# The expert stage's sixteen slots: waiting slot by slot instead of by groups of four

## The reference, cut to what matters

```python
def one_block(args):
    hb, eb, gb = args
    a = jax.nn.gelu(jnp.einsum('td,thkd->thk', hb, u[eb]))
    return jnp.einsum('thk,thkd->td', (gb * a).astype(v.dtype), v[eb])
```

## Time and profile before

| | us |
|---|---|
| median of three runs | 5759.28 (5758.3 to 5764.06) |
| profiled execution, its own time | 5768.66 |
| its span, first to last instruction | 5766.5 |
| TensorE busy in the span | 4560.9 (79%) |
| VectorE busy | 2323.8 (40%) |
| GpSimd busy | 1169.3 (20%) |
| ScalarE busy | 886.2 (15%) |
| queue of the gathers (q0), its packets' time as a share of 16 engines' span | 46.0% |

### The profile page before, as it was taken

How to read it: one execution, slowest core, us unless ns; L and a number is a source line. 1 busy time by engine, 2 the same in 40 slices (tenths; PEclk the granted TensorE clock), 3 DMA queues, 4 the chain that set the end, 5 groups by cost and what they waited for, 6 DMA issues and landing times. The chain is left out here.

```text
span 5766.5 us, 41916 instructions
## 1 busy us (share of the span) xinstructions
PE 4560.9 (79%) x13011; PEld 2177.4 (38%) x13044; DVE 2323.8 (40%) x5481; ACT 886.2 (15%) x1951; POOL 1169.3 (20%) x1104
## 2 busy tenths in 40 slices
PE   6999999977777767888837777777777777777777
PEld 1444444434544543344312333333333333333333
DVE  2000000003333334388894554454544445454544
ACT  1100000012222220121101111111111111111111
POOL 0000000000000000000004444444444444444443
PEclk8999999987777776899977888888888898889888
DMA  7143444462101023311009999999999999999997
GB/s 260 53 156 136 149 156 156 166 208 92 42 35 57 31 76 136 140 47 47 28 3 367 411 409 412 405 402 400 407 401 401 407 408 412 408 411 410 410 405 313
DMA packets 247745, 1409.28 MB, mean 244 GB/s; under 512 B 24467, under 2 KB 76179, under 8 KB 110804
## 3 DMA queue, kind: packets, MB, share of 16 engines
q0 software_dynamic: 148896, 1083.11, 46.0%
q1 hardware_dynamic: 72118, 272.53, 13.4%
q10 hardware_dynamic: 26672, 52.88, 2.4%
HBM read 1341.66 MB, written 159.08 MB: 260 GB/s over the span
## 5 line engine op out<-in xcount | busy, mean ns | idle before, releaser
L1677 DVE CUSTOM_DVE_ANT_0 ex_UV<-ex_UV,ex_h 128x1024 f32<-128x1024 f32 x1024 | 1194.0, 1221 | 1211.9 <-DMA ex_UV<-in_peer_uv,ex_idx 1211.9
L1546 POOL DMA_INDIRECT ex_UV<-in_peer_uv,ex_idx x1024 | 1135.0, 1108 | 1534.5 <-PE ex_acc L1591 630.5
L1591 PE MATMUL ex_acc<-ex_UV,ex_diag 128*128 128x512 f32 x2048 | 1015.8, 659 | 320.2 <-ACT ex_diag L1617 320.2
L1591 PE MATMUL ex_bc<-ex_UV,ex_diag 128*128 128x512 f32 x2048 | 1008.9, 656 | 318.1 <-ACT ex_diag L1617 318.1
L406 PE MATMUL z_ps<-win,hT 128*128 128x464 f32 x2688 | 1055.2, 554 | 22.3 <-ACT z_stage L383 11.6
L1591 PEld LDWEIGHTS ex_acc<-ex_UV,ex_diag 128*128 128x128 f32 x2048 | 429.3, 213 | 905.8 <-issue 526.6
L1591 PEld LDWEIGHTS ex_bc<-ex_UV,ex_diag 128*128 128x128 f32 x2048 | 425.9, 211 | 899.7 <-issue 519.6
L406 PEld LDWEIGHTS z_ps<-win,hT 128*128 128x128 f32 x2688 | 510.9, 191 | 555.9 <-issue 537.4
L763 DVE TENSOR_SCALAR mx_gn<-mx_gn 128x1024 f32<-128x1024 f32 x1 | 0.7, 694 | 1136.8 <-DMA mx_gn<-in_gla_gn_g 1136.8
L1534 POOL DMA_INDIRECT ex_UV<-in_peer_uv,ex_idxT x8 | 7.6, 953 | 1740.9 <-DVE ex_idxT L1646 1738.8
L1612 ACT ACTIVATE ex_u<-ex_u 128x8 f32<-128x8 f32 x128 | 26.7, 209 | 2130.0 <-DVE ex_u L1449 2130.0
(11 more groups left out here) (332 smaller groups left out, 3399.5 us busy)
## 6 DMA issues: line engine op xcount, KB each, us to landing
out_kv_w_sample<-in_cache_kv_w SPq DMA_DIRECT2D x8, 8188.0 KB, 42.7
win<-in_w_in SPq DMA_DIRECT2D x21, 1856.0 KB, 11.4
z_scratch<-z_stage ACTq DMA_DIRECT2D x21, 1856.0 KB
ada<-in_ada_w SPq DMA_DIRECT2D x12, 2048.0 KB, 7.8
ex_UV<-in_peer_uv,ex_idx POOLq DMA_INDIRECT x1024, 8.5
out_kv_w_sample<-in_cache_kv_w SPq DMA_DIRECT2D x8, 2044.0 KB, 18.1
mx_zg<-z_scratch SPq DMA_DIRECT2D x8, 1544.0 KB, 7.1
mx_zq<-z_scratch SPq DMA_DIRECT2D x8, 1536.0 KB, 10.1
```

The costliest lines, as they stand in the source:

```text
L1546: pool.indirect_dma_start(out=UV[n][:, :], out_offset=None, in_=uv_dram, in_offset=bass.IndirectOffsetOnAxis(ap=idx[b][:, n:n + 1], axis=0 ...
L1591: last = nc.tensor.matmul(acc[:, b, :], dg[:, n, :], V[n][:, b * 512:(b + 1) * 512], start=False, stop=False)
L1677: nc.vector.tensor_tensor_reduce(out=U[n], in0=U[n], in1=hb, scale=1.0, scalar=0.0, op0=ALU.mult, op1=ALU.add, accum_out=a[:, n:n + 1]).th ...
```

## The change

The landing semaphores become sixteen, one per slot. GpSimd waits before every gather for one more slot to be summed. VectorE waits before every dot and TensorE before every sum for that slot's own landing. Names `NBUF` (16), `ROUNDS` (`NSLOT // NBUF`, 1), `SUB` (8) and `SUBS` (2) replace literal values; buffers are addressed as `n % NBUF`.

```diff
-    GRP = 4
-    NQ = NSLOT // GRP
-    HALF = NSLOT - NS
+    NBUF = 16
+    ROUNDS = NSLOT // NBUF
+    HALF = NBUF - NS
...
-    loaded = [k.sem(f"ex_rows_loaded{q}") for q in range(NQ)]
+    loaded = [k.sem(f"ex_slot_loaded{n}") for n in range(NBUF)]
...
-    SUB = NSLOT // 2
+    SUB = 8
+    SUBS = NSLOT // SUB
...
                     for n in range(NSLOT):
-                        if n % GRP == 0:
-                            pool.wait_ge(p["vdone"], (i * PH + h) * NSLOT + n + GRP)
-                            pool.sem_inc(p["zero"], 1)
-                        pool.indirect_dma_start(out=UV[n][:, :], out_offset=None, in_=uv_dram,
-                                                in_offset=bass.IndirectOffsetOnAxis(ap=idx[b][:, n:n + 1], axis=0)).then_inc(loaded[n // GRP], 16)
+                        pool.wait_ge(p["vdone"], (i * PH + h) * NSLOT + n + 1)
+                        pool.sem_inc(p["zero"], 1)
+                        pool.indirect_dma_start(out=UV[n % NBUF][:, :], out_offset=None, in_=uv_dram,
+                                                in_offset=bass.IndirectOffsetOnAxis(ap=idx[b][:, n:n + 1], axis=0)).then_inc(loaded[n % NBUF], 16)
...
-                            if n % GRP == 0:
-                                pe.wait_ge(loaded[n // GRP], (i * PH + h) * (16 * GRP) + 16 * GRP)
+                            pe.wait_ge(loaded[n % NBUF], ((i * PH + h) * ROUNDS + n // NBUF) * 16 + 16)
...
-                            if n % GRP == 0:
-                                dve.wait_ge(loaded[n // GRP], (i * PH + h) * (16 * GRP) + 16 * GRP)
+                            dve.wait_ge(loaded[n % NBUF], ((i * PH + h) * ROUNDS + n // NBUF) * 16 + 16)
...
-                        at_least(dve, p["diag"], (i * PH + h) * NSLOT + c * SUB - SUB)
+                        at_least(dve, p["diag"], (i * PH + h) * NSLOT + c * SUB + SUB - NSLOT)
```

More of the change, by code:

```diff
@@ L1462, in experts @@
     rows_s = [k.sem(f"ex_rows_sample{n}") for n in range(NS)]
-    loaded = [k.sem(f"ex_rows_loaded{q}") for q in range(NQ)]
+    loaded = [k.sem(f"ex_slot_loaded{n}") for n in range(NBUF)]
     uv_dram = k.i["peer_uv"]
-    SUB = NSLOT // 2
+    SUB = 8
+    SUBS = NSLOT // SUB
     with k.phase() as f:
-        UV = [f.sb(f"ex_UV{n}", [P, 2 * D]) for n in range(NSLOT)]
+        UV = [f.sb(f"ex_UV{n}", [P, 2 * D]) for n in range(NBUF)]
         U = [t[:, 0:D] for t in UV]
@@ L1576, in _ @@
                 pe.wait_ge(s["s_sum"], 1)
-                pe.sem_inc(p["vdone"], NSLOT - HALF)
+                pe.sem_inc(p["vdone"], NBUF - HALF)
                 pe.wait_ge(s["tiles_done"], 2)
@@ L1586, in tile @@
                         for n in range(NSLOT):
-                            if n % GRP == 0:
-                                pe.wait_ge(loaded[n // GRP], (i * PH + h) * (16 * GRP) + 16 * GRP)
+                            pe.wait_ge(loaded[n % NBUF], ((i * PH + h) * ROUNDS + n // NBUF) * 16 + 16)
                             pe.wait_ge(p["diag"], (i * PH + h) * NSLOT + n + 1)
                             for b in range(2):
-                                last = nc.tensor.matmul(acc[:, b, :], dg[:, n, :], V[n][:, b * 512:(b + 1) * 512], start=False, stop=False)
+                                last = nc.tensor.matmul(acc[:, b, :], dg[:, n, :], V[n % NBUF][:, b * 512:(b + 1) * 512], start=False, stop=False)
                             last.then_inc(p["vdone"], 1)
@@ L1609, in head @@
                 def head(i, h):
-                    for c in range(2):
-                        act.wait_ge(p["g_u"], (i * PH + h) * 2 + c + 1)
+                    for c in range(SUBS):
+                        act.wait_ge(p["g_u"], (i * PH + h) * SUBS + c + 1)
                         nc.scalar.activation(uu[:, c * SUB:(c + 1) * SUB], uu[:, c * SUB:(c + 1) * SUB], ACT.Tanh, scale=GELU_C).then_inc(p["g_exp"], 1)
-                        act.wait_ge(p["w"], (i * PH + h) * 2 + c + 1)
+                        act.wait_ge(p["w"], (i * PH + h) * SUBS + c + 1)
                         for n in range(c * SUB, (c + 1) * SUB):
@@ L1671, in head @@
                 def head(i, h, hb):
-                    for c in range(2):
+                    for c in range(SUBS):
                         cols = slice(c * SUB, (c + 1) * SUB)
                         for n in range(c * SUB, (c + 1) * SUB):
-                            if n % GRP == 0:
-                                dve.wait_ge(loaded[n // GRP], (i * PH + h) * (16 * GRP) + 16 * GRP)
-                            nc.vector.tensor_tensor_reduce(out=U[n], in0=U[n], in1=hb, scale=1.0, scalar=0.0, op0=ALU.mult, op1=ALU.add,
+                            dve.wait_ge(loaded[n % NBUF], ((i * PH + h) * ROUNDS + n // NBUF) * 16 + 16)
+                            nc.vector.tensor_tensor_reduce(out=U[n % NBUF], in0=U[n % NBUF], in1=hb, scale=1.0, scalar=0.0, op0=ALU.mult, op1=ALU.add,
                                                            accum_out=a[:, n:n + 1]).then_inc(p["dotted"], 1)
@@ L1680, in head @@
                         dve.sem_inc(p["dots_done"], SUB)
-                        link = chained(dve, p["g_steps"], (i * PH + h) * 6 + c * 3)
+                        link = chained(dve, p["g_steps"], ((i * PH + h) * SUBS + c) * 3)
                         gelu_steps(nc, link, a[:, cols], t[:, cols], uu[:, cols]).then_inc(p["g_u"], 1)
-                        dve.wait_ge(p["g_exp"], (i * PH + h) * 2 + c + 1)
+                        dve.wait_ge(p["g_exp"], (i * PH + h) * SUBS + c + 1)
                         link(nc.vector.scalar_tensor_tensor(out=t[:, cols], in0=uu[:, cols], scalar=1.0, in1=a[:, cols], op0=ALU.add, op1=ALU.mult))
                         gate = k.gate[:, bass.ds(i * P + h * NSLOT + c * SUB, SUB)]
-                        at_least(dve, p["diag"], (i * PH + h) * NSLOT + c * SUB - SUB)
+                        at_least(dve, p["diag"], (i * PH + h) * NSLOT + c * SUB + SUB - NSLOT)
                         nc.vector.scalar_tensor_tensor(out=w[:, cols], in0=t[:, cols], scalar=0.5, in1=gate, op0=ALU.mult, op1=ALU.mult).then_inc(p["w"], 1)
```

## The result

| | before | after |
|---|---|---|
| median | 5761.42 us (5758.3 to 5764.06, 4 runs) | 5681.43 us (5674.33 to 5687.88, 4 runs) |
| ratio | | 0.9861, 95% interval 0.9844 to 0.9878 |
| profiled execution, span | 5768.66, 5766.5 | 5674.33, 5672.2 |
| first gather of the stage to the last instruction | 2739.9 us | 2645.3 us |

The changed kernel is 1.4% faster. The prediction said 5668 (5648 to 5722). Run beside another kernel later, it had 5678.03 (5 runs) against 5767.32 (9 runs) before, ratio 0.9846 (0.9826 to 0.9865).

A forecast was written before the change was run, and what follows sets the result against it. Gathers bound the expert stage, losing 94 us to a short queue. From 5768.66 us: -94, 6 given back, -3 at the end, giving 5678; the median lies 9.4 us below that execution, so 5668 us (5648 to 5722).

The forecast's parts named there:

- What bounds it: Expert stage, 3100 to 5730 us: gathers move 407 GB/s against 422 with a filled queue; 94 us lost.
- (1) to (3): Finer refill and landing waits: first refill issued 7.7 us into a turn instead of 17.9, reserve 11.2 us, gaining 94 us.
- T: Instant in one turn of the loop when VectorE starts on the last group of a half's slots as its landing is seen.
- (4): Price of the added waits, 768 each on VectorE, TensorE and GpSimd: taken as 0, being met or covered.
- The upper bound of 353 us: Cost of the added waits if uncovered: 768 at 0.46 us each.
- (5): VectorE's tail of a tile, some 6.5 us, seven times between heads 0 and 1: covered by the reserve of 11.2 us.
- (6): Ends of the stage: start as before; after the last landing one dot instead of four, 3.4 us less.
- A: Rival: the short queue is filled only in part, half of the 94 us returns, 5709 us; chance 0.14.
- B: Rival: nothing moves, 407 GB/s is what scattered rows give, only the end gains, 5756 us; chance 0.08.
- C: Rival: dots slow GpSimd's gathers, its issuing becomes the bound at 2.74 us per gather, +174 us, 5933; chance 0.05.
- D: Rival: TensorE becomes the bound, half of its matmuls at 0.86 us, all of them +890 us; chance 0.03.
- Signs: Expected in the trace: 420 GB/s or more, VectorE's waits near 1100 us in some 1000 pieces, GpSimd's longest below 6.

The follow-up runs named there:

- only the waits: Kernel before, with its group's wait repeated before every slot on GpSimd, TensorE and VectorE, 768 more met waits on each: 5770.16 us, ratio 1.0001.
- refill alone: Kernel before, with only GpSimd's waits changed to one more sum before each gather, landings still counted by four: 5681.28 us, ratio 0.9854.
- landing alone: Changed kernel, with GpSimd again waiting for four sums before each fourth gather, landings still slot by slot: 5679.02 us, ratio 0.9852.
- landings by eight: Kernel before, with landings counted by eight and GpSimd waiting for one more sum before every gather: 5772.88 us, ratio 1.0013.
- half the bytes: Changed kernel, each gather fetching 4 KB per row instead of 8, v rows not fetched: 4890.68 us.
- early release: Changed kernel, with the sample's sum run slot by slot, freeing each of slots 8 to 15 at once: 5679.52 us beside 5678.03 us for the changed kernel.

## Why the prediction was right, step by step

**What bounds it.** Right. The 94 us of a short queue, read from GB/s, were there to be won: 422 GB/s throughout, and the stage 94.6 us shorter, 3.5 of it after the last landing and 91 before. I had given 6 us back for tails and first heads; about 3 were lost. These 3 us are less than two executions differ: the kernel with only the waits, whose steady part is that of before, has a stage of 2733.3 us, 6.6 less than before. The second of the two figures of the Trainium skill that the prediction weighed ("HBM Reference", section Specifications (TRN2): about 425 GB/s for a core that streams alone) agrees with the 422 that the filled queue holds for 2540 us; the first, a share of 358, doesn't bind here.

**(1) to (3).** T+3.5, T+8.1 and a reserve of 10.4 us against the predicted T+3.5, T+7.7 and 11.2. What the prediction said of the turn before, "The queue was empty", is more than its rows show: the DMA share in the earlier trace rows is 0.71 and 0.72, and the reserve there was 0.6 to 1.0 us. A short queue loses time before it is empty: of the 89 us that the kernel before lost in its steady halves, nearly all fell in halves with a reserve below 2.5 us, and none in the others. The prediction also left out that the steps are no sum. It presented both as parts of one gain of 94 us; refill alone and landing alone each bring all of it.

**(4)** The value taken, 0, is what the kernel with only the waits measured: 1.0001 (0.9990 to 1.0012). The upper bound of 353 us is excluded. The cover was named rightly: one copy and its wait more per gather on GpSimd, and the time rises.

**(5)** Seven tails cost nothing visible: no stretch of 20 us between 3100 and 5620 falls below 418 GB/s.

**(6)** The end gave 3.5 us, as worked out. The start is unchanged at 0.61 of DMA share; how it is tied to VectorE I hadn't seen.

**The size.** In the profile 5674.33 against a forecast sum of 5678. The medians give 80 to 89 us less than before, not 91, with the start of the stage moving by up to 20 us from one execution to the next. The forecast of 5668 lies 13 us below the measured median, no more than the four runs differ among themselves (5674 to 5688).

**A and B** didn't come about; B's claim, that 407 is what scattered rows give, is refuted. **C**: half right as a mechanism. Dots do slow the gathers, to 1.99 us, and with landings by eight that was one part, not the largest as far as the traces tell, of a loss of the whole gain; but I had read the row of 10.37 us as the price of eight dots in a row, and that reading is wrong. **D**: TensorE is the next bound, but it doesn't come near: with half the bytes, where it doesn't wait, its granted clock is 1.00. That fewer pauses would raise the clock of the changed kernel did not show: 0.88 before and after.

**Signs.** VectorE's waits (1040.2 us in 863 pieces) and the end came as written. GpSimd's longest wait for TensorE did not: 10.7 us instead of below 6. It waits after its last refill, with a full queue behind it, and a wait with a full queue costs nothing.

## What to carry to other kernels

Where a ring of buffers feeds from a transfer queue, follow one turn: when is the first buffer released, when is its transfer in the queue, and when does the queue run out? The difference is the reserve; below zero it costs its full size every turn, below the time of one transfer (2.5 us here) it still costs a part, and above that nothing more can be gained, so any one of several edits may bring it all. Judge a transfer bound by bytes per second against the best stretch of the same trace, not by the busy share.

## What the runs showed of the hardware that I had not expected

The gather that takes 10.37 us stands once per execution, the fifth after the sample's sum, beside the first eight dots of the prompt (10.38 in the kernel with landings by eight; with a copy after each gather it is the third, 11.01 us), and is missing only with early release. Chains of eight dots elsewhere hold a gather for 2.0 us at most. The Trainium skill ("SBUF — State Buffer", section SBUF: two separate sides) says that a VectorE operation which holds the shared port keeps GpSimd from writing descriptors; the 1.99 instead of 0.94 us fit that, the 10.37 isn't explained by it alone, and its cause stays open.

A queue with one or two gathers in it, never empty, ran at 396 GB/s over 10 us instead of 422. And the text ahead of the stage, the same in all kernels, took up to 20 us more or less from one execution to the next.

GpSimd's pause comes at fixed intervals in the changed kernel too: every 98th gather comes 2.4 to 3.6 us after the one before it, with nothing in the profile that it waits for. There the reserve of 5 us or more hides it. Its cause stays open.

A landing is seen later in a full queue. From a gather's last packet to the update of its semaphore it was 2.5 us (median) in the changed kernel and 1.1 in the one with landings by eight. So a reserve that is counted to the landings seen looks 1 to 2.5 us larger than it is.
